# A two-block transformer kernel: routing's norm, transposes and scores moved into the second output product, a shorter recurrence step, and constants loaded inside the norm stage

## The reference

```
hx/hc = modulate(rmsnorm(x or ctx, norm1_g), shift, scale)   # "norm stage": 2 blocks of ctx, 8 of x
p = h @ w_in;  r, k, v, decay, a, gate = split and shifted p
y = rwkv_bidir(...)        # a recurrence over 1280 tokens, forward and backward, 8 heads of 64
a_x = rwkv_out(y, ...);  b_x = short_conv(...)
x = x + g1 * (concat([a_x, b_x]) @ w_out)                    # second output product
hx = modulate(rmsnorm(x, norm2_g), sh2, sc2)                 # routing's norm
aff = softmax(hx @ router_w)                                 # scores, 16 experts
vals, idx = top_k(aff.T, 128);  x = x + g2 * expert_choice_ffn(...)
out = rmsnorm(x, final_g)
```

## Time and profile before

| What | us |
|---|---|
| median of 3 runs (lowest 3002.74, highest 3013.65) | 3004.51 |
| the profiled execution's own time | 3004.86 |
| its span in the profile | 3003.1 |
| norm stage with its constants and columns | 1014 to 1086 |
| recurrence | 1545 to 2065 |
| second output product | 2129 to 2243 |
| routing (norm, scores, softmax, search, tables) | 2243 to 2388 |
| experts | 2388 to 2969 |
| final norm | 2969 to 3003 |

### The profile page before, as it was taken

One profiled execution on the slowest core, in us unless ns is written; L12 is line 12 of the kernel. 1 busy time (PEld: TensorE's weight loads), 2 busy tenths in 40 slices (PEclk: granted clock), 3 DMA queues, 4 the chain that ended last, 5 costly groups with the idle time before them and its releaser, 6 DMA issues. The chain is left out here.

```text
span 3003.1 us, 56691 instructions
## 1 busy us (share of the span) xinstructions
PE 2475.9 (82%) x23638; PEld 1885.2 (63%) x23638; DVE 1637.8 (55%) x2058; ACT 989.9 (33%) x1552; POOL 633.9 (21%) x618
## 2 busy tenths in 40 slices
PE   4698997959998469999858878888676299999993
PEld 1487654537676458887326767775465188888882
DVE  2793447721114332466455555553424899999993
ACT  2121442220103230000334333333102177777772
POOL 0221347302110013221034444440000010100000
PEclk8799999979999769999559999997695599999996
DMA  9232003421103211110141011101435199999993
GB/s 381 70 137 76 21 1 114 119 102 35 52 21 136 100 56 57 64 36 22 67 133 30 19 25 25 31 12 42 173 109 188 44 408 407 388 394 399 398 380 133
DMA packets 132727, 405.61 MB, mean 135 GB/s; under 512 B 55090, under 2 KB 64946, under 8 KB 102690
## 3 DMA queue, kind: packets, MB, share of 16 engines
q1 hardware_dynamic: 119268, 359.53, 31.9%
q0 software_dynamic: 4608, 16.78, 2.3%
q10 hardware_dynamic: 8640, 26.19, 2.2%
HBM read 346.85 MB, written 55.61 MB: 134 GB/s over the span
## 5 line engine op out<-in xcount | busy, mean ns | idle before, releaser
L3070 DVE TENSOR_TENSOR ex_wl<-ew_raw,ex_wh 128x2048 fp32r<-128x2048 f32 x192 | 435.5, 2289 | 42.5 <-ACT ex_wh L3032 39.0
L3032 ACT ACTIVATE ex_wh<-ew_raw 128x2048 fp32r<-128x2048 f32 x192 | 367.5, 1919 | 110.0 <-PE ex_U L2976 40.3
L125 PE MATMUL sp_acc<-b2h_hi,sp_wh 128*128 128x512 f32 (+1 forms) x528 | 194.9, 369 | 11.8 <-POOL sp_wl L1614 11.8
L125 PE MATMUL sp_acc<-b2h_lo,sp_wh 128*128 128x512 f32 (+1 forms) x528 | 194.6, 369 | 0.0
L125 PE MATMUL sp_acc<-b2h_hi,sp_wl 128*128 128x512 f32 (+1 forms) x528 | 194.5, 368 | 0.0
L2162 ACT ACTIVATE rc_xt<-rc_ps 128x256 f32<-128x256 f32 x200 | 67.7, 389 | 192.1 <-PE rc_ps L2331 191.6
L2953 POOL DMA_INDIRECT x<-ex_o,ex_at x16 | 26.5, 1656 | 494.1 <-DVE ex_o L3093 494.1
L1100 DVE TENSOR_TENSOR merge_sg<-b_pj,merge_sg 128x512 f32<-128x512 f32 x16 | 11.1, 693 | 218.2 <-ACT merge_sg L1086 218.2
L2229 DVE TENSOR_TENSOR rc_x<-rc_x,rc_ps 128x256 f32<-128x256 f32 x160 | 60.1, 417 | 120.7 <-PE rc_ps L2317 120.5
L125 PE MATMUL merge_acc<-merge_hh,merge_wh 128*128 128x512 f32 x256 | 101.5, 397 | 26.4 <-POOL merge_wl L119 21.1
L1612 POOL CAST sp_wh<-sp_w 128x1024 fp32r<-128x1024 f32 x26 | 27.1, 1042 | 434.2 <-DMA sp_w<-in_w_conv 250.2
(11 more groups left out here) (471 smaller groups left out, 6278.9 us busy)
## 6 DMA issues: line engine op xcount, KB each, us to landing
ew_raw<-in_exp_gate SPq DMA_DIRECT2D x64, 1024.0 KB, 8.1
ew_raw<-in_exp_up SPq DMA_DIRECT2D x64, 1024.0 KB, 9.4
ew_raw<-in_exp_down SPq DMA_DIRECT2D x64, 1024.0 KB, 8.1
b_pj<-in_ada_w SPq DMA_DIRECT2D x24, 1024.0 KB, 18.9
rc_ac<-ac SPq DMA_DIRECT2D x40, 256.0 KB, 4.1
merge_w<-in_w_merge SPq DMA_DIRECT2D x16, 512.0 KB
ac<-rp_ac SPq DMA_DIRECT2D x4, 2048.0 KB, 7.1
pr_w<-in_w_main SPq DMA_DIRECT2D x14, 512.0 KB
```

The costliest lines, as they stand in the source:

```text
L125: ins = nc.tensor.matmul(out, w[a][:, k, :], h[b][:, k, cols], start=(first and n == 0), stop=(last and n == 2))
L3032: nc.scalar.activation(wh[:, n % RING], raw[:, n % RING], ACT.Copy).then_inc(q["w_hi"], 1)
L3070: V.tensor_tensor(wl[:, n % RING], raw[:, n % RING], wh[:, n % RING].bitcast(f32), ALU.subtract).then_inc(q["w_lo"], 1)
```

## The change

Five edits are made together.

1. `affine_columns` is gone. `mixer_norms` loads the modulation rows and the norm's gain first, makes `ab` in the same phase, ahead of the second block, and issues the other constants from SP just before the load of block 6.
2. In the recurrence ACT copies only the crossed half to `g`; DVE adds the state's half straight from PSUM, so `solved` has one term instead of two. PE's multiplies of `kst` are cut in two halves around `advanced(0)`, `right_side_of_state` comes behind them, `outputs` comes behind `advanced(1)`, and the turning of the rows behind `products(2)`. The four adds to `y` are interleaved over the directions.
3. The second output product becomes `out_scored`. `aT` and `bT` come in halves. Behind each block's residual, norm, scaling, transposes and scores of that block run in the same loop, from the tile and without reading `x2` back; the transposes stand on PE inside the next block, the scores inside the one after it. The stores go through SP.
4. `route` starts with the softmax, from a small tile `scores`.
5. `final_norm` takes mean and root block by block behind each square, has eight slots of `y`, and loads the gain's row behind the first block.

```diff
 def mixer_norms(...)
             def _(sp):
+                for dst, src in ((rows[:], mod_rows), (n1[:], n1_row)):
+                    sp.dma_start(dst, src).then_inc(q["rows_loaded"], 16)
                 for b in range(N):
+                    if b == 6:
+                        for dst, src in constants:
+                            sp.dma_start(dst, src).then_inc(q["constants_loaded"], 16)
...
             def _(dve):
+                    if b == 1:
+                        dve.wait_ge(q["rows_turned"], 1)
+                        for row in range(2):
+                            V.tensor_scalar(ab[:, 2 * row, :], pc[:, KD:, row], 1.0, None, ALU.add).then_inc(q["ab_made"], 1)
...
 def rwkv_chunks(...)                                   # ACT
-                        A.activation(paired(b["g"][:]), crossed(2, d), ACT.Copy).then_inc(s["g_ready"], 1)
-                        A.activation(b["gs"][:], stayed(2, d, 1), ACT.Copy).then_inc(s["g_ready"], 1)
+                        copy("g_crossed", i, lambda b: paired(b["g"][:]), lambda d: crossed(2, d), "g_copied")
...
+                def right_side(count):                 # DVE
                     for d in range(2):
+                        dve.wait_ge(joint["g_done"], count)
+                        V.tensor_tensor(b["g"][:], stayed(2, d, 1), b["g"][:], ALU.add).then_inc(s["g_ready"], 1)
...
                 def body(i, sl, half, old, here, following):
                     masked(i, 0)
                     advanced(i, 0, sl)
+                    if old is not None:
+                        right_side(i)
                     masked(i, 1)
+                    factor(i, sl, 0)
                     advanced(i, 1, sl)
+                    factor(i, sl, 1)
                     masked(i, 2)
...
                     x_turned(i, 0, sl)                 # PE
                     if old is not None:
                         right_side(i, 1 - sl)
-                        right_side_of_state(i, 1 - sl)
-                    advanced(i, 0, sl)
...
-                    crossing(3, 2 * CK, (...)).then_inc(joint["pk_done"], 1)
+                    keys(sl, 0)
+                    advanced(i, 0, sl)
+                    keys(sl, 1).then_inc(joint["pk_done"], 1)
+                    if old is not None:
+                        right_side_of_state(i, 1 - sl)
                     x_turned(i, 1, sl)
                     products(i, 1, sl)
                     if old is not None:
                         solved(i, 1 - sl)
                     advanced(i, 1, sl)
+                    if old == "all":
+                        outputs(i, 1 - sl)
+                    x_turned(i, 2, sl)
+                    products(i, 2, sl)
...
+def out_scored(nc, T, I, halves, w_dram, split, x_dram, mod_dram, y_dram, h_dram, scores):
+            def _(sp):
+                for k in range(KD):
+                    if k < NP:
+                        half(k, 0)
+                    if k == 4:
+                        for i in range(NP):
+                            half(i, 1)
+                    if k >= 4:
+                        sp.wait_ge(q["w_lo"], k - 3)
+                    sp.dma_start(w[:, k % 4, :], w_dram[:, k, :]).then_inc(w_loaded[k % 4], 16)
+                    if k < 2:
+                        x_load(k)
+                for dst, src in ((row[:], ...), (a_row[:], ...), (b_row[:], ...), (xn[:, 0, :], I["norm2_row"])):
+                    sp.dma_start(dst, src.to_broadcast([P, D])).then_inc(q["rows_loaded"], 16)
...
+                for b in range(NB):                    # PE
+                    for k in range(KD):
+                        if k == 2 and b >= 2:
+                            scored(b - 2)
+                        if k == 6 and b >= 1:
+                            turned(b - 1)
+                        # six multiplies of 128x512
+                scored(NB - 2)
+                turned(NB - 1)
+                scored(NB - 1)
...
+                for b in range(NB):                    # ACT
+                    if b + 2 < NB:
+                        put(b + 2)
+                    act.wait_ge(q["added"], b + 1)
+                    nc.scalar.activation(xn[:, s, :], y[:, s, :], ACT.Square, accum_out=st[:, 0, b:b + 1])
+                    nc.scalar.activation(st[:, 2, b:b + 1], st[:, 1, b:b + 1], ACT.Sqrt)
+                    for h in range(2):
+                        act.wait_ge(q["turned"], 2 * b + h + 1)
+                        nc.scalar.activation(hT[:, k, :], pt[:, k, :], ACT.Copy).then_inc(q["hT_ready"], 1)
...
+                    if b + 1 < NB and b:               # DVE
+                        put(b + 1)
+                    V.tensor_tensor(yb, acc[:, s].rearrange("p h n -> p (h n)"), row[:], ALU.mult)
+                    V.tensor_tensor(yb, yb, xt[:, s, :], ALU.add).then_inc(q["added"], 1)
+                    V.tensor_scalar(st[:, 1, b:b + 1], ...); V.reciprocal(st[:, 3, b:b + 1], ...)
+                    V.scalar_tensor_tensor(xn[:, s, :], yb, st[:, 3, b:b + 1], a_row[:], ALU.mult, ALU.mult)
+                    V.tensor_tensor(xn[:, s, :], xn[:, s, :], b_row[:], ALU.add).then_inc(q["normed"], 1)
...
 def final_norm(...)
-        y = ph.sb("y", [P, 2, D])
+        y = ph.sb("y", [P, NB, D])
...
                 for b in range(NB):
+                    if b + 1 < NB:
+                        mean(b + 1)
+                    dve.wait_ge(q["rooted"], b + 1)
+                    V.reciprocal(st[:, 3, b:b + 1], st[:, 2, b:b + 1]).then_inc(q["inverted"], 1)
...
                     V.scalar_tensor_tensor(y[:, b, :], x[:, b, :], st[:, 3, b:b + 1], row[:], ALU.mult, ALU.mult)
```

More of the change, by code:

```diff
@@ L1166, in put @@
                 def put(b):
+                    if late and b in (0, NB // 2):
+                        act.wait_ge(q["late1" if b else "late0"], 16 * len(late))
                     if b >= 2:
@@ L1552, in _ @@
             def _(pe):
+                pe.wait_ge(q["rows_loaded"], 32)
+                for k in range(2 * KD):
+                    last = nc.tensor.transpose(pc[:, k, :], rows[:, k * P:(k + 1) * P], T.ident[0:2, 0:2])
+                last.then_inc(q["rows_turned"], 1)
                 for b in range(N):
@@ L2303, in _ @@
                 chunks(dve, body)
+                right_side(NCK)
                 outputs(NCK - 1)
@@ L2308, in _, with crossing @@
                 M = nc.tensor.matmul
-                def crossing(n, w, *terms):
-                    for j, s in product(range(HP // 2), range(2)):
+                def crossing(n, w, *terms, pairs=range(HP // 2)):
+                    for j, s in product(pairs, range(2)):
                         for i, (l, r) in enumerate(terms):
```

396 lines of the change are left out of this document (226 added, 170 removed).

## The result

The changed kernel takes 2922.45 us (median of 4 runs, 2913.5 to 2926.26), the kernel before in the same comparison 3006.4 us (4 runs, 3002.74 to 3013.65). The ratio is 0.9714, with a 95% interval of 0.9683 to 0.9744: 2.9% faster. The forecast of 2910 was 12 us low, inside its range. The profiled execution took 2919.78 us, of which 2917.8 are the span.

What follows compares the result with a forecast made beforehand. No single bound: stages run one after another, each with its own limit. Terms -16.7 - 28 - 42 - 7.5 = -94.2 against the profiled 3004.86 us gave 2910 us, range 2888 to 2945.

Steps and rivals of the forecast that it cites:

- Norm stage: Norm opening: first block issued and squared earlier, constants loaded before block 6 at no cost; -16.7 us, bounds -13 and -17.
- Output product and routing: Second output product and routing fused: blocks of 13.6 us, softmax sooner after the last; -42 us, bounds -20 and -47.
- Rival D: Fused output loop bound by a DVE-ACT-PE chain, 3 us waiting per block: +21, 2931 us; with part of B, chance 0.12.
- B: Fused output loop at 1.2 GHz throughout: whole gain gone, 3005 us, chance 0.02; a fifth of that gives 2929.
- Final norm: Final norm: first root after two squares, then a block each 1.75 us; -7.5 us, bounds -4 and -9.
- Recurrence: Recurrence: 1.4 us less in each of 20 steps; -28 us, bounds -8 and -46.
- the walk: One recurrence step traced through in the new order with profiled durations, giving 1.3 to 1.4 us less a step.
- the state's multiplies fill DVE's time behind it: Recurrence, behind advanced(0): advanced(0) starts 0.9 us earlier and the second product at 4.9 for 5.2.
- it no longer waits for four copies: Recurrence's solve: 32 multiplies for 64 (-0.5 us) and no wait for ACT's four copies.
- `outputs` fills DVE's time: Recurrence, behind advanced(1), where the turning of rows stood before; level 2 starts its advanced at 10.1 for 11.3 us.
- Rival A: Recurrence's gain returns as late instructions, limited by PE's own 20.6 us and gaps: 0.4 a step, 2930 us; chance 0.15.
- Rival C: Recurrence: DVE's wait for g_done stalls its queue and shifts later levels; 4.3 us more a step gives 3024; chance 0.03.

Runs made afterwards that it cites:

- e6: Changed kernel with all 32 of the keys' multiplies ahead of advanced(0), as before; ratio 0.974, recurrence 504.9 us.
- e7: Changed kernel with the second half of the keys' multiplies moved behind the second product, ahead of the solve; ratio 0.9718, recurrence 502.4 us.
- e5: Changed kernel with the solve's 32 multiplies issued twice over; ratio 0.9769, recurrence 514.7 us.
- four unshifted runs: New recurrence order with no transposes added ahead of it: the changed kernel, e3, e4 and e10; recurrence 501.6 to 507.0 us.
- e2: Changed kernel with the old norm opening, constants and affine columns in their own phases; ratio 0.9735, 2926.3 us, recurrence 494.5 us.
- e1: Changed kernel with the recurrence's old function put back; ratio 0.9761, 2934.0 us, recurrence 515.8 us.
- shift of 64: 64 tiny transposes at the head of PE's recurrence: changed kernel, ratio 0.9704, recurrence 513.9 us; kernel before, ratio 0.9993, recurrence 510.0 us.
- shift of 8: e10's kernel with 8 tiny transposes at the head of PE's recurrence; ratio 0.9696, 2908.9 us, recurrence 494.9 us.
- e3: Changed kernel with the old second output product and old routing phase; ratio 0.9849, 2962.2 us.
- e4: Changed kernel with the old final norm, one root for all blocks and two output slots; ratio 0.9769, 2933.4 us.
- e10: Changed kernel with the product inputs' second halves loaded last and two tables loaded ahead by dummy operations; ratio 0.9745, 2917.5 us.
- shift of 32: e10's kernel with 32 tiny transposes at the head of PE's recurrence; ratio 0.974, 2923.5 us, recurrence 514.7 us.

## Why the prediction was right where it was, and where it was not

Behind each head stand the forecast and the measured difference, in us; the latter is from one profiled execution on each side.

**Norm stage** (-16.7, was -16.5): right by its steps. First square forecast at 1018.6, found at 1017.95, in a stage that began 0.8 earlier; block 6 in time.

**Output product and routing** (-42, was -42.8): right by its sum and nearly by its steps. The opening's two parts were divided otherwise (block 0 was gated at 33.1 us instead of 29.2, since the rows landed late; PE had gone on meanwhile and waited 1.06 us for `normed`, not 3), but both hang on the rows' landing, and the end of block 1 is the same. Blocks 13.63, scores 1.85, transposes 1.03 to 1.09. Behind it the table load and the slots' landing cost 1.3 where I put 1; the 1.5 us that the tables gave back by a higher clock, and with them the stage's last microsecond, are luck. Rival D did not come, nor B: the clock stayed at 1.00. The Trainium skill (TensorE: Matmul & The Clock Gate, Part 4: PE-mode transpose) has transposes count as no activity; 1 us of them in 13.6 did no harm here.

**Final norm** (-7.5, was -8.4): right; scalings follow each other in 1.45 us for the 1.75 that I gave, so the last comes 10.1 us after the first and not 11 to 14, against a first scaling that came later, at 9.9 us for 8.9, for the late second block and the table.

**Recurrence** (-28, was -15.2): the mis-sized term. The mechanism was half right. The full steps gained 0.75 us each for the 1.4 of the walk, about what the removed multiplies (0.5) and fewer or shorter gaps can give. What failed is the walk's rest: "the state's multiplies fill DVE's time behind it", "it no longer waits for four copies", "`outputs` fills DVE's time". It took some 0.9 us of waiting out of each step, but PE's waits other than late instructions were 1.19 us before and 1.25 after. I priced each piece that was moved off the path at what it had taken there, and took its new place for free. But such a place is about as long as DVE's 0.75 with its hand-overs, and I put 1.6 us of PE's work into it: the first `advanced` came 0.93 earlier, and the second `masked`, which I had 0.3 earlier (the second product at 4.9 for 5.2), not at all. `e6` and `e7` show the same from both sides: PE's work moved by one place shifts the events between, and the step by 0.2 us or less. They are the firmest of these runs, since they leave the count of PE's instructions, and so the place of all that follow, as it was. `e5` points the same way but moves the places too. A changed step is PE's 20 us of busy time, 2.6 of late instructions and 1.2 of other waits; `e7` cut PE's wait for the mask by 0.4 of these and gained nothing.

Rival A named the late instructions, and gave 0.4 a step. It had the right bound, PE's own work and the gaps; but the gaps did not take the gain back, they fell from 3.03 to 2.57 us a step. The measured 0.76 (15.2 over twenty steps) lies between its price and the walk's. Rival C, the wait for `g_done`, did not show: DVE's add began 1.5 us ahead of the second mask.

How much of the 15.2 belongs to the order of instructions at all is less sure than the four unshifted runs make it look. 5.9 of it come ahead of the end of the first step, which my walk did not price, and which ends after 39.6 to 44.7 us in kernels with the same recurrence. That new recurrence as a whole took 494.5 to 514.7 us by what stands ahead of it, the old one 510.0 to 518.5. Against the 518.5 of before that is a gain of 4 to 24 us, so that the term fell inside its bounds of 8 to 46 is in part luck. The kernel before is itself at another place than the changed one: the new norm opening takes 8 PE records away ahead of the recurrence (12375 before, 12367 after, by the traces). Compared at the same place, the new order gains 24 us at 12375 (518.5 against `e2`'s 494.5), 12 at 12367 (`e1`'s 515.8 against 504, the mean of the unshifted four), and at a shift of 64 it loses 4 (510.0 against 513.9, places 8 apart).

The means of the places tried (old: 518.5, 515.8 and 510.0; new: 504, 494.5, 494.9, 514.7, 513.9) are 514.8 and 504.4. Their difference, 10 us, is near to the 8.6 that twenty times 0.43 of removed work would give; but the busy time of the same 701 records itself went from 19.8 to 20.4 us a step over these kernels, so the agreement shows little.

## What to carry to other kernels

Where an engine is busy for over 80% of a loop's step and most of the rest is gaps with no releaser, as here, look for instructions to take away; moving them into another engine's waiting time counts only by how much of that time is really empty, so add up all that already stands there. A load moved out of the way, or a table loaded ahead, is worth nothing until you have found what lands next: look up the second-latest release before pricing the latest, and ask whether a longer wait will cost the clock. And the length of a dense loop of small multiplies is only known to within some 2% either way from one placement (494.5 to 514.7 us here); time it with its code shifted before you credit an order with less than that.

## What the runs showed that I had not expected

The instructions' placement. In the fifteen full steps, TensorE stood idle with nothing to wait for during 1.93 to 3.11 us a step, in 2.7 to 4.6 gaps of 0.6 to 0.9 us on average and up to 2.5. The page of the changed kernel has the queue that fetches instructions:

```profile
q8 instruction: 165, 2.70, 0.4%
```

That is 16 KB each (2.70 MB in 165 packets). The trace ties the gaps to these pieces. Number all of PE's records in order of time, weight loads, multiplies and its sequencer's: in the changed kernel all 49 gaps of the fifteen steps stand at the same place of a count of 256, within 4 records, so that the distances between them are close to 256, 512, 768 or 1024. In each of the other kernels such places hold 96 to 100% of the gaps' time, also where a shift had moved the code against the count. In the same stretch the queue moves 85 packets, and 85 times 256 records pass (88 and 88 before). So an instruction comes late only where a new piece of 256 begins, in 49 of 85 cases there, by 0.8 us on average.

That explains how a shift can change the loop: it moves these places within the steps. Eight transposes more (16 instructions) changed it by -7 us against the unshifted 501.6, 32 or 64 by +10 or more. The old norm opening of `e2` moved the count by 8, and its 494.5 us agree with the 494.9 of the shift of 8. It also shows how little fewer instructions save by this: 63 records fewer a step are a quarter of a piece, at 0.5 us each some 0.13 of the 0.46 (an estimate from the 45.3 us of gaps over 88 pieces before). The rest is where the pieces begin. Why one place costs nothing and another up to 2.5 us stays open. The Trainium skill (Runtime: NRT & Kernel Launch, Instruction fetch mechanics) has the fetch mostly hidden by the pace of issue; these rows disagree, for multiplies of 64 x 64 that start every 0.015 us (32 in 0.5).

The stage behind the recurrence, which the change leaves alone, took from 53.6 to 66.3 us with the same 120 matmul records. Its windows in the kernel with a shift of 64, and in the one with a shift of 8:

```profile
2046.22:2099.77 53.55, 46.27 (x120) 20.23 (x120) 19.70 (x31) 14.45 (x23) 0.00 (x0) 0.66 0.23 84
```

```profile
2025.71:2091.98 66.27, 58.99 (x120) 27.28 (x120) 19.69 (x31) 14.45 (x23) 0.00 (x0) 0.53 0.19 68
```

The granted clock is 0.66 in the one, 0.53 in the other, and 0.59 in the changed kernel (60.1 us): time at 2.4 GHz against time at 1.2 GHz in a stage where PE keeps pausing. So a few microseconds won in the recurrence can be lost here, or the other way round, and the two stages together are the better measure: 563.4 us changed, 577.0 with the old recurrence, 581.3 before, 572.9 before with a shift of 64. By this measure the three other unshifted kernels (`e3`, `e4`, `e10`) have 563.0 to 569.0, the shift of 8 has 561.1 and that of 64 has 567.5, inside their range, as its runs said; only `e2` (553.6) and the shift of 32 (575.0) stand well apart.
